# Joining the opening products of the delta rule, which share their weights, to matmuls of 128 moving columns

## What is computed

```python
def step(S, inp):
    r_t, w_t, k_t, v_t, kk_t, b_t = inp
    sa = jnp.einsum('bhvk,bhk->bhv', S, -kk_t)
    S = (S * w_t[:, :, None, :] + sa[..., None] * b_t[:, :, None, :]
         + v_t[..., None] * k_t[:, :, None, :])
    return S, jnp.einsum('bhvk,bhk->bhv', S, r_t)
```

## Time and profile before

| | |
|---|---|
| three runs | 1228.95, 1229.07, 1227.23 us; median 1228.95 |
| the profiled execution | 1226.94 us, its span 1225.1 us |
| busy in the span | PE 97%, PEld 87%, DVE 67%, ACT 42%, POOL 7% |
| clock granted to TensorE, mean | 0.992 of full |
| mixing part of interest | 550.8 to 675.7 us from the span's start |

### The profile page before, as it was taken

The page is one execution under the profiler, slowest core; times in us unless marked ns, Lnnn a source line. Parts: engine busy times, 40 slices in busy tenths (PEclk is TensorE's granted clock), DMA queues, the critical chain, the costliest instruction groups (busy, mean ns, idle before and its releaser), DMA issues.

```text
span 1225.1 us, 29536 instructions
## 1 busy us (share of the span) xinstructions
PE 1183.5 (97%) x12538; PEld 1068.6 (87%) x12538; DVE 820.4 (67%) x1155; ACT 512.1 (42%) x794; POOL 90.3 (7%) x89
## 2 busy tenths in 40 slices
PE   9999999999999999998988998999999999999996
PEld 8999999999999988885546445698999999999995
DVE  4875895699557555254664553787885797679754
ACT  5432442244334755343543434334733244244333
POOL 0000000000020210000450021010000000000021
PEclk9999999999999999999999999999999999999998
DMA  6223222223213767645665998641222222323211
GB/s 226 91 91 130 104 95 95 104 104 104 104 36 121 295 223 241 225 156 188 222 211 160 293 314 295 241 174 38 102 95 95 104 104 91 134 75 106 97 36 71
DMA packets 56725, 177.38 MB, mean 145 GB/s; under 512 B 7186, under 2 KB 7443, under 8 KB 47251
## 3 DMA queue, kind: packets, MB, share of 16 engines
q1 hardware_dynamic: 53426, 169.48, 40.6%
q10 hardware_dynamic: 3168, 6.02, 1.4%
HBM read 164.64 MB, written 10.83 MB: 143 GB/s over the span
## 4 chain that ended last, share of the span: by engine, by line
PE 90%; DVE 6%; issue 2%; ACT 2%; DMA 1%; SPq 0%; DVEq 0%; POOL 0%; ACTq 0%; POOLq 0%
PE banks L387 36%; PE banks L592 30%; PE banks L1295 3%; PE banks L2105 2%; PE banks L2035 2%; PE banks L2323 2%; PE banks L410 2%; PE banks L1042 2%; PE banks L2277 1%; PE banks L1588 1%; PE banks L2183 1%; PE banks L2398 1%; PE banks L920 1%; PE banks L2197 1%; PE banks L907 1%
## 5 line engine op out<-in xcount | busy, mean ns | idle before, releaser
L366 DVE TENSOR_TENSOR weights_lo<-weights_raw,weights_hi 128x1024 fp32r<-128x1024 f32 (+1 forms) x90 | 106.8, 1196 | 97.9 <-ACT weights_hi L358 97.2
L358 ACT ACTIVATE weights_hi<-weights_raw 128x1024 fp32r<-128x1024 f32 (+1 forms) x90 | 90.8, 1018 | 164.4 <-PE banks L387 142.5
L387 PE MATMUL banks<-hidden_hi,weights_hi 128*128 128x260 f32 x576 | 116.3, 283 | 0.0
L387 PE MATMUL banks<-hidden_hi,weights_lo 128*128 128x260 f32 x576 | 115.5, 282 | 0.0
L387 PE MATMUL banks<-hidden_lo,weights_hi 128*128 128x260 f32 x576 | 115.5, 282 | 0.0
L387 PE MATMUL banks<-x_hi,weights_hi 128*128 128x260 f32 x544 | 111.2, 286 | 0.0
L387 PE MATMUL banks<-x_hi,weights_lo 128*128 128x260 f32 x544 | 109.6, 283 | 0.0
L387 PE MATMUL banks<-x_lo,weights_hi 128*128 128x260 f32 x544 | 109.3, 282 | 0.0
L387 PEld LDWEIGHTS banks<-x_hi,weights_hi 128*128 128x128 f32 x544 | 83.7, 188 | 12.6 <-issue 11.7
L592 PE MATMUL banks<-x_sums_hi,more_weights_hi 128*128 128x260 f32 x320 | 90.6, 283 | 0.0
L592 PE MATMUL banks<-x_sums_hi,more_weights_lo 128*128 128x260 f32 x320 | 90.5, 283 | 0.0
(11 more groups left out here) (409 smaller groups left out, 3014.2 us busy)
## 6 DMA issues: line engine op xcount, KB each, us to landing
cache_pages<-in_cache_k SPq DMA_DIRECT2D x128, 256.0 KB, 3.6
weights_raw<-in_gate_up_b SPq DMA_DIRECT2D x22, 1024.0 KB, 4.7
weights_raw<-in_gate_up_a SPq DMA_DIRECT2D x21, 1024.0 KB, 4.8
cache_pages<-in_cache_v SPq DMA_DIRECT2D x56, 256.0 KB, 3.7
weights_raw<-in_w_in SPq DMA_DIRECT2D x13, 1024.0 KB, 5.9
projected<-in_cache_v SPq DMA_DIRECT2D x48, 256.0 KB, 3.8
weights_raw<-in_down_a SPq DMA_DIRECT2D x8, 896.0 KB, 4.6
weights_raw<-in_down_b SPq DMA_DIRECT2D x8, 896.0 KB, 4.6
```

The lines of the kernel that those rows point to most:

```text
L358: nc.scalar.activation(WH[pr.slot(i, k)][:, 0:nk, :], RAW[slot][:, 0:nk, P * (k % 2):P * (k % 2) + P], ACT.Copy).then_inc(split_hi, 1)
L366: nc.vector.tensor_tensor(WL[pr.slot(i, k)][:, 0:nk, :], RAW[slot][:, 0:nk, P * (k % 2):P * (k % 2) + P], WH[pr.slot(i, k)][:, 0:nk, :].bi ...
L387: mm = nc.tensor.matmul(acc[s][:, a, 0:HALF], w[slot][:, t, :], x[:, k0 + t, HALF * a:HALF * a + HALF], start=begins and t == tiles[0] and ...
```

## The change

`TT` and `RBT` have the same weights `FB`, and `MT` and `RKT` the same weights `FK`. The change puts `FA` and `FR` of each `i` into one tensor `receptances_and_keys` [128, 6, 512] in which they lie three rows apart, and multiplies both at once:

- `T+R` takes the place of `TT` and `RBT`, `M+R` of `MT` and `RKT`: 16 matmuls each, of the same weights with 2 x 64 = 128 moving columns, into the same pair of banks side by side. VectorE still makes one masked multiplication per output, both under one `take`.
- In the first opening `T` goes ahead of `T+R`, and the wait for both accumulators is split: `T0` waits for `acc_free[0]`, `T+R0` for `acc_free[1]`.
- `OPENED_AT` becomes: `T+R2` at 5, `T+R3` at 6, `M+R2` at 7, `T2 T3` before the late products, `M+R3` behind them and then both decode groups.

```diff
-                     4: (("tokV", 3), ("tokA", 3)), 5: (("TT", 2),), 6: (("TT", 3),), 7: (("MT", 2),),
-                     "before": (("T", 2), ("MT", 3)),
-                     "behind": (("T", 3), ("RBT", 2), ("RKT", 2), ("RBT", 3), ("RKT", 3))}
+                     4: (("tokV", 3), ("tokA", 3)), 5: (("T+R", 2),), 6: (("T+R", 3),), 7: (("M+R", 2),),
+                     "before": (("T", 2), ("T", 3)), "behind": (("M+R", 3),)}
...
+        def spread_both(pe, name, lhs, both):
+
+            ring_free(pe, name)
+            for j in range(4):
+                for h, p in ((0, 0), (1, 1), (0, 1), (1, 0)):
+                    rows, cols = slice(64 * h, 64 * h + 64), slice(P * j + 64 * p, P * j + 64 * p + 64)
+                    mm = nc.tensor.matmul(side_by_side(name)[64 * p:64 * p + 64, h, :, 64 * j:64 * j + 64], lhs[rows, cols],
+                                          both[rows, :, cols], start=True, stop=True)
+            ring_full(mm)
...
         def opening_tensor(pe, two, before):
             if not before:
-                for i in two:
-                    for n in ("TT", "T"):
+                pe.wait_ge(acc_free[0], outp.used0[0])
+                opened_tensor(pe, ("T", two[0]))
+                pe.wait_ge(acc_free[1], outp.used0[1])
+                opened_tensor(pe, ("T+R", two[0]))
+                for i in two[1:]:
+                    for n in ("T", "T+R"):
                         opened_tensor(pe, (n, i))
...
                 for i in two:
-                    for n in ("MT", "RBT", "RKT"):
-                        opened_tensor(pe, (n, i))
+                    opened_tensor(pe, ("M+R", i))
...
             if nxt:
                 for name in OPENED_AT["behind"]:
                     opened_tensor(pe, name)
-                    if name[0] == "RKT":
-                        decode(pe)
+                    decode(pe, 2)
```

More of the change, by code:

```diff
@@ L253, in layer @@
         LG2 = LORA
-        FEATURES = sb("features", [P, 6, SEQ])
-        FA, FB, FK = ([FEATURES[:, 2 * n + u, :] for u in range(2)] for n in range(3))
+        FEATURES = sb("features", [P, 4 * TOK])
+        FB, FK = ([FEATURES[:, SEQ * (2 * n + u):SEQ * (2 * n + u + 1)] for u in range(2)] for n in range(2))
+        RARAR = sb("receptances_and_keys", [P, 6, SEQ])
+        FA, FR = ([RARAR[:, n, :] for n in at] for at in ((2, 3), (0, 1, 4, 5)))
+        FAR = [RARAR[:, i:i + 3:2, :] for i in range(4)]
         class Chunks:
@@ L267, in layer @@
         ML = Chunks([MIXED[:, c, :] for c in (2, 3, 6, 7)] + [MIXED_EARLY[:, 2, :], MIXED_EARLY[:, 3, :], MIXED[:, 4, :], MIXED[:, 5, :]])
-        FR = [sb(f"r_features{i}", [P, SEQ])[:, :] for i in range(2)] + FR2
         FACTOR = Y[:, 7, :]
@@ L1438, in ring_order @@
                     for i in two:
-                        add_opening(*((n, i) for n in ("MT", "RBT", "RKT")))
+                        add_opening(("M+R", i))
                 for i in before:
@@ L1755, in products_pool @@
             pool.wait_ge(g("decays"), i + 1)
-            full(pool, ("RKT", 1))
+            full(pool, ("M+R", 1))
             pool.tensor_tensor(FA[u][:, :], KN[:, 0:SEQ], CUM[:, 0:SEQ], ALU.mult)
@@ L2412, in opened_tensor @@
                 turned(pe, name, {"tokB": FB[u], "tokK": FK[u], "tokV": pj(20 + i)[:, 0:SEQ]}[kind])
-            else:
-                lhs, rhs = {"TT": (FB[u], FA[u]), "T": (FA[u], FB[u]), "MT": (FK[u], FA[u]),
-                            "RBT": (FB[u], FR[i]), "RKT": (FK[u], FR[i])}[kind]
-                spread(pe, name, lhs, rhs)
+            elif kind == "T":
+                spread(pe, name, FA[u], FB[u])
+            else:
+                spread_both(pe, name, {"T+R": FB, "M+R": FK}[kind][u], FAR[i])
         def opening_tensor(pe, two, before):
             if not before:
-                for i in two:
-                    for n in ("TT", "T"):
+                pe.wait_ge(acc_free[0], outp.used0[0])
[4 more added lines that the diff above has]
+                    for n in ("T", "T+R"):
                         opened_tensor(pe, (n, i))
@@ L2562, in chain_tensor @@
                     opened_tensor(pe, name)
-                    if name[0] == "RKT":
-                        decode(pe)
+                    decode(pe, 2)
         def phase_tensor(pe, a, b, before, nxt):
-            if not before:
-                projected(pe)
             opening_tensor(pe, (a, b), before)
@@ L2825, in bonus_terms_vector, with masked_out @@
                                            op1=ALU.mult).then_inc(g("bonus_terms"), 1)
-        def masked_out(dve, name, out, mask):
-            take(dve, name)
-            was_read(nc.vector.tensor_tensor(heads(out), heads(two_banks(name)[:, :, 0:256]), masked(mask), ALU.mult), name)
+        def masked_out(out, name, side, mask):
+            return nc.vector.tensor_tensor(heads(out), heads(side_by_side(name)[:, :, side, :]), masked(mask), ALU.mult)
         def bonus_vector(dve, i):
@@ L2862, in opened_vector @@
             n, i = name
-            out, mask = {"TT": (TT, C_STRICT), "T": (PP, C_LOW1), "MT": (MT, C_STRICT), "RBT": (RBT, C_INCL), "RKT": (RKT, C_INCL)}[n]
-            masked_out(dve, name, out[i % 2], mask)
+            u, keys = i % 2, int(i < 2)
+            take(dve, name)
+            if n == "T+R":
+                masked_out(TT[u], name, keys, C_STRICT)
+                was_read(masked_out(RBT[u], name, 1 - keys, C_INCL), name)
+            if n == "M+R":
+                masked_out(MT[u], name, keys, C_STRICT)
+                was_read(masked_out(RKT[u], name, 1 - keys, C_INCL), name)
             if n == "T":
+                was_read(masked_out(PP[u], name, 0, C_LOW1), name)
                 was_taken(dve, name)
@@ L2871, in opening_vector @@
                 for i in two:
-                    for n in ("TT", "T"):
+                    for n in ("T", "T+R"):
                         opened_vector(dve, (n, i))
                 for i in two:
-                    for n in ("MT", "RBT", "RKT"):
-                        opened_vector(dve, (n, i))
+                    opened_vector(dve, ("M+R", i))
                 return
```

12 lines of the change are left out of this document (5 added, 7 removed).

## The result

The changed kernel takes **1220.76 us** (median of 12 runs, 1217.92 to 1227.12), the kernel before 1228.56 us (12 runs) on the same chip: ratio 0.9945, 95% interval 0.9929 to 0.9961. The profiled execution took 1217.92 us with a span of 1216.1; the one before 1226.94 and 1225.1.

The account below looks back on a forecast made before the run. The prediction took TensorE as the bound, with late instruction packets and half clock costing time in both openings. It summed 4.9 + 4.7 - 1.2 = 8.4 us off the mean 1228.05, giving 1219.7 us, range 1216.5 to 1224.5.

Parts of the forecast that it names:

- What bounds the kernel, and what the gaps are: TensorE bounds; its unexplained gaps in both openings are instruction packets arriving late, 2.14 and 1.66 us, each with half clock behind.
- Joined matmuls alone: Both openings: 16 single spreads at 0.58 us become 8 joined at 1.05, saving 0.9 us of TensorE time.
- First opening, head: From T0 to tokA: 0.1 us later, the split wait's early start being used up by receptances' masks moved forward.
- First opening, tail: From M+R0 to the turns: 4.9 us won, 1.7 by fewer masks, the rest by gap and half clock gone.
- Second opening: Up to centered: 4.7 us won (gap 1.66, half clock 1.7, fewer spreads 1.3), less 1.2 for a possible new gap.
- The sum: Whole kernel: 4.9 + 4.7 - 1.2 = 8.4 us won, giving 1218.5 profiled and 1219.7 us forecast.
- rival 4: Edges shift and a later gap (at 641.8, 759.8 or 763.8) closes too: 1218.3 us and below; chance 0.07.
- A gap that comes back (1): One gap returns in full with half clock, likelier in the second opening: 1222 to 1223.5 us; chance 0.25.
- Gaps tied to the work (2): Gaps are not a matter of supply and stay at their work; only 3.0 us won, 1225.0 us; chance 0.12.
- Slower (3): An edge falls on joined spreads in steps 5 to 7, both old gaps staying: 1229 us and above; chance 0.04.
- Value pages (5): Behind the second opening, page transfers limit, so its gain does not arrive: 4.9 us alone, 1223.2 us; chance 0.04.

Follow-up runs that it names:

- the second control by 256: Changed kernel with 256 records more in the warm-up, by the cheaper padding of 16-column products, so edges lie where they were: 1222.0 us, ratio 0.9933.
- the edges moved by 64: Changed kernel with 64 TensorE records more in the warm-up, every packet edge 64 records earlier: 1225.4 us, 1222.5 less the late start.
- the single products: Changed kernel with each of its eight joined products written as two of 64 moving columns, same order, banks and masks: 1224.9 us, ratio 0.9985.
- the last one: Changed kernel with joined products written as two of 64 columns each and edges 176 records earlier: 1222.7 us, ratio 0.9954.
- the old one with its edges moved: Kernel before with 128 records more in the warm-up, by the cheaper padding of 16-column products, work unchanged: 1225.4 us, ratio 0.9965.

## Why the prediction was right

**What bounds the kernel, and what the gaps are.** Right, and shown by moving the edges alone. By the Trainium skill, "Runtime: NRT & Kernel Launch", "Instruction fetch mechanics", a block's edge is mostly hidden. That holds for most edges here, and for the block size, but not for the dense blocks: the largest gap at an edge is 1.0 to 2.6 us in every kernel of this study, 2.32 us in the changed one. One step was weak: ten packets in 70.70 us give a mean of 7 us, and the gap behind a block of 4.9 us shows how little that says of a single one.

**Joined matmuls alone** (0.9 us). A joined spread takes 1.10 us with its tail, two take 1.98 back to back, so 1.0 each where 1.05 was taken. At equal edges joining is worth 0.7 us by the medians and 1.6 by the ratios, a difference smaller than their intervals.

**First opening, head** (0.1 later; without the split 0.8 more). Measured 0.17 later, and 0.86 more without it.

**First opening, tail** (4.9 us). `M+R0` at 563.61 (563.5 predicted), `Y(0,0)` at 566.21 (566.2), turns at 568.03 (568.0), ended 569.12: 4.84 us. The load of the gates begins at 569.59 in the chain (569.5) against the earlier trace rows.

**Second opening** (4.7 us, less 1.2 for a new gap). `centered` at 666.46, where 4.9 + 4.7 give 666.1 without a new gap and 667.3 with it. The timeline has no idle time at that edge, inside the decode groups at about 665.5, and both groups take 2.3 us, where two alone take 2.0: the 1.2 us were mis-sized and are at most 0.3 in this execution. In three others (the second control by 256, the one without the split wait, the one with the first opening alone joined) a gap of 0.54, 0.34 and 0.60 us stands there, and the groups take 3.4, 3.2 and 3.5 us; so this edge sits near the bound.

**The sum.** 8.4 us; the medians say 7.8, the profiled executions 9.0. The predicted 1219.7 lies 1.1 us below the median; this is smaller than the spread of the runs, and the two later gaps, which I had left as they were (1.44 us at 761.4 and 1.2 at 765.2 in the kernel before), were 0.75 and 2.32 here. The profiled execution agrees with 1218.5 to 0.6 us.

The two openings were foretold step by step; that the rest adds up to so little is in part luck. Matmul for matmul, the changed kernel leads by 4.8 us behind the first opening. It loses 1.5 of that at 578.81, to a half clock that the kernel before does not have there, and wins 1.2 where the old gap at 641.8 is gone; neither was in the sum (the second was part of rival 4). At `centered` it leads by 9.2, behind 0.5 us of page waits and the two later gaps by 8.1. The last 0.9 comes in the last group of TensorE, which takes 2.23 instead of 3.10 us: in the kernel before the clock falls to half inside it (at 1213.1), in the changed one behind it (at 1206.9).

**The rivals.** A gap that comes back (1) is what the edges moved by 64 made, and the single products: 1222.5 and 1224.9 us. Gaps tied to the work (2) is refuted. Slower (3) did not happen at any edge that was tried: less the late start, all ten variants of the new order lie at 1221 to 1225 us. More won (4) came true in part: the gap at 641.8 of before (1.2 us) is not among the changed kernel's waits, but the later pair is 0.4 us longer and the half clock at 578.81 took more back. Value pages (5): 0.5 us of waits in the changed kernel, 1.4 to 2.5 in five experiments, 7.8 in the profiled execution of the last one; not the bound here, but the next one.

So of some 8 us (the kernel before lay in the five sets at 1227.5 to 1229.1), by the medians some 3.4 come with the new order, masks and split wait, singles kept (1224.9), and 4.2 with joining; by the ratios it is 1.8, with an interval from nothing to 4.2, and 4.9. Of the part of joining 0.7 to 1.6 remains when the edges lie elsewhere; the other 3.3 or so is the gap and the half clock at one edge.

No version that was run is told apart from the changed kernel on the fast side.

## What to carry to other kernels

Where an idle time of TensorE has no engine to blame, count the records between such gaps: if they are multiples of 250 or so, and a packet of the instruction queue moves in each gap, the packets are late, and the remedy is fewer, longer matmuls in the dense stretch. Before crediting an edit of a dense stretch, move the edges alone (some small products in the warm-up, with a control by a whole 256): here that was worth 3 to 4 us to the old kernel, half of what the change brought. When forecasting where an edge will bite, count every block of the stretch and not only the one that bit before, and treat a block as short as the 4.9 us seen here as at risk.

## What the runs showed that I had not expected

- The half clock does not follow each gap. Behind 2.32 us (757.12, changed kernel), 1.16 us (668.67) and 0.99 us (568.55) the granted clock stayed at 1.00; behind 1.02 us (557.71, single products) it fell to 0.50 for 3.4 us. Behind gaps of 2.59 us at one and the same product it stayed in one kernel (763.12, the second control by 256) and fell in another (763.76, the first opening alone joined). It also fell once at 372.5, 1.8 us behind an idle time of 0.68 us (the second control by 256), and, beginning between 577 and 587, in the changed kernel and ten of the twelve experiments, for 3.4 or 6.8 us. No gap at an edge stands there, but TensorE waits for VectorE: in the changed kernel 1.45 us up to 578.09, and at 578.81 the clock falls. The kernel before has the same 1.45 us up to 582.94 and keeps its clock. So of the 1.7 us that I had added to each gap a part is chance. These are the rows of the changed kernel and of the old one with its edges moved, behind their gaps:

```profile
757.10:761.00 3.90, 3.88 (x50) 1.76 (x50) 2.17 (x6) 1.71 (x3) 0.00 (x0) 1.00 0.89 281
568.60:572.60 4.00, 3.57 (x112) 2.98 (x116) 2.05 (x4) 1.09 (x2) 0.00 (x0) 1.00 0.04 15
```

- Small products of 64 x 64 weights in one and the same quarter of the array cost 0.11 us each (70 in 7.67 us), and the products behind them stayed slow for longer than behind the large ones that they replaced: with 140 of them the multiplication began at 16.24 us with products of 0.80 and 0.64 us, still 0.64 at 20.3 us, which take 0.40 in the changed kernel from 8.75 us on. That the clock was low there is inferred from these durations.
